# A pool-and-retention decoder step: two independent panels put into each head of the sample stage, states loaded one by one

## What is computed

```python
h = rmsnorm(x, g_norm)
u_p, z_p, q, k, v, z_r, gates = split(h @ w_in)            # w_in: 1024 x 10240
pooled = window_mean(u_p with 15 old rows, 2/4/8/16) - u_p # four groups of 256 columns
y_pool = ((pooled @ w_pool_group) * pool_scale * silu(z_p)) @ w_branch_pool
for each of 4 heads:                                       # q, k: 256 wide, v: 512 wide
    o, s_new = retention(rope(q), rope(k), v, state_ret)   # state: 8 sequences x 256 x 512
    y_ret += (group_norm(o) * gn_ret * silu(z_r)) @ w_branch_ret
merged = sigmoid(gate_p) * y_pool + sigmoid(gate_r) * y_ret
y_sample = rmsnorm(x + merged @ w_out, g_final)
```

## Time and profile before

| | us |
|---|---|
| median of 3 runs | 3111.87 (3109.57 to 3117.58) |
| the profiled execution, its own time | 3111.35 |
| its span, first to last instruction | 3109.7 |
| mean granted TensorE clock | 0.989 |
| PE busy | 2991.4 (96%) |
| sample stage, first panel to last instruction | 2783.36 to 3103.0 |

### The profile page before, as it was taken

The page is one execution under the profiler, slowest core; times in us unless marked ns, Lnnn a source line. Parts: engine busy times, 40 slices in busy tenths (PEclk is TensorE's granted clock), DMA queues, the critical chain, the costliest instruction groups (busy, mean ns, idle before and its releaser), DMA issues.

```text
span 3109.7 us, 36004 instructions
## 1 busy us (share of the span) xinstructions
PE 2991.4 (96%) x13000; PEld 2305.5 (74%) x13000; DVE 1826.3 (59%) x2594; ACT 1152.4 (37%) x1892; POOL 712.1 (23%) x499
## 2 busy tenths in 40 slices
PE   6999999999999999999998999999999999999997
PEld 5888887877778888887887788788888888772222
DVE  7666665764454656666664674657567566754331
ACT  4444443444454444443443333333334332322210
POOL 4252535343332334343432000000000000001110
PEclk8999999999999999999999999999999999999999
DMA  4535353435553354444445546735654663559895
GB/s 131 198 127 190 124 195 129 176 122 183 178 175 122 136 177 148 165 159 150 156 162 220 223 163 246 276 121 193 242 193 161 237 270 140 193 173 336 298 310 190
DMA packets 297599, 582.06 MB, mean 187 GB/s; under 512 B 24840, under 2 KB 167688, under 8 KB 286255
## 3 DMA queue, kind: packets, MB, share of 16 engines
q1 hardware_dynamic: 292039, 562.73, 51.1%
q0 software_dynamic: 5392, 17.12, 1.5%
HBM read 410.63 MB, written 169.50 MB: 187 GB/s over the span
## 4 chain that ended last, share of the span: by engine, by line
PE 84%; DVE 7%; DMA 3%; issue 3%; ACT 2%; POOL 1%; SPq 0%; DVEq 0%; ACTq 0%; POOLq 0%
PE bank L1134 24%; PE bank L1136 24%; PE bank L1135 24%; PE bank L1426 7%; PE bank L1464 2%; PE bank L1182 1%; DMA raw<-in_w_branch_pool 1%; DVE z_in L2123 1%; DVE wa_lo L1857 1%; DMA xs<-in_x_prompt 1%; DVE z_lo L1857 1%; PE bank L1457 1%; DVE win_a L1857 1%; PE bank L1129 1%; DVE c_out L1857 1%
## 5 line engine op out<-in xcount | busy, mean ns | idle before, releaser
L1134 PE MATMUL bank<-xa_hi,wa_hi 128*128 128x512 f32 x2240 | 887.4, 396 | 16.4 <-DVE c_out L1857 11.8
L1136 PE MATMUL bank<-xa_hi,wa_lo 128*128 128x512 f32 x2240 | 877.2, 392 | 0.0
L1135 PE MATMUL bank<-xa_lo,wa_hi 128*128 128x512 f32 x2240 | 876.5, 391 | 0.0
L1134 PEld LDWEIGHTS bank<-xa_hi,wa_hi 128*128 128x128 f32 x2240 | 423.5, 189 | 103.8 <-issue 19.2
L1136 PEld LDWEIGHTS bank<-xa_hi,wa_lo 128*128 128x128 f32 x2240 | 423.0, 189 | 89.2
L1135 PEld LDWEIGHTS bank<-xa_lo,wa_hi 128*128 128x128 f32 x2240 | 423.8, 189 | 85.1
L1857 DVE TENSOR_TENSOR wa_lo<-w_raw,wa_hi 128x512 fp32r<-128x512 f32 x320 | 308.9, 967 | 209.0 <-ACT wa_hi L1559 207.9
L1857 DVE TENSOR_TENSOR wa_lo<-w_sum,wa_hi 128x512 fp32r<-128x512 f32 x240 | 189.4, 789 | 226.7 <-ACT wa_hi L1559 226.7
L1857 DVE TENSOR_TENSOR w_lo<-raw,w_hi 128x512 fp32r<-128x512 f32 (+1 forms) x288 | 180.0, 658 | 228.1 <-ACT w_hi L1665 228.0
L1559 ACT ACTIVATE wa_hi<-w_raw 128x512 fp32r<-128x512 f32 x320 | 201.1, 628 | 243.4 <-PE bank L1136 243.4
L1665 ACT ACTIVATE w_hi<-raw 128x512 fp32r<-128x512 f32 (+1 forms) x288 | 165.5, 603 | 280.3 <-PE bank L1136 108.5
(11 more groups left out here) (238 smaller groups left out, 4606.8 us busy)
## 6 DMA issues: line engine op xcount, KB each, us to landing
w_raw<-in_w_in SPq DMA_DIRECT2D x80, 1024.0 KB, 5.1
v_d<-turned SPq DMA_DIRECT2D x64, 512.0 KB, 3.2
qk_s<-qk_d SPq DMA_DIRECT2D x32, 1024.0 KB, 7.0
v_s<-v_d SPq DMA_DIRECT2D x32, 1024.0 KB, 10.8
raw<-in_w_branch_ret SPq DMA_DIRECT2D x128, 256.0 KB, 4.2
s_w<-in_w_in SPq DMA_DIRECT2D x64, 512.0 KB, 5.0
tabs<-in_c_rope SPq DMA_DIRECT2D x16, 1024.0 KB, 5.2
qk_d<-high SPq DMA_DIRECT2D x32, 512.0 KB, 4.5
```

The costliest lines, as they stand in the source:

```text
L1134: pe.matmul(out, lh, rh, start=first, stop=False, skip_group_check=onto)
L1135: pe.matmul(out, lh, rl, start=False, stop=False, skip_group_check=onto)
L1136: return pe.matmul(out, ll, rh, start=False, stop=last, skip_group_check=onto)
```

## The change

- PE, ACT, DVE and POOL write out the loop over heads; thresholds become constants and the `waited` increments go.
- Two panels from the part after the heads stand in each head between z and the transposes of `s_og`: u0, u1 in head 0, zp0, zp1 in head 1, gp0, gp1 in head 2, gr0, gr1 in head 3 (banks 2 and 0). The transposes of u stand behind v of head 1, the pool groups' product behind v of head 3, the transposes of `s_mix` ahead of those of `s_og` in head 3. ACT and DVE get the work on these results in the same heads.
- SP loads states of the next head one by one, each behind the ACT step that scaled its old buffer: four ahead of this head's branch loads, four behind them. So the next head's states stand ahead of its qk and v loads. The gate bias and pool scale are loaded at the end of head 0.
- PE's waits for `fills` and `hist_copied` stand ahead of head 0's first panel, once, and no more behind each v panel.

```diff
@@ semaphore places
+PANELS = []
+for _h, _others in enumerate((("u0", "u1"), ("zp0", "zp1"), ("gp0", "gp1"), ("gr0", "gr1"))):
+    PANELS += [("qk", _h), ("v", _h)] + [("mix", None)] * (_h == HEADS - 1) + [("z", _h)]
+    PANELS += [(name, None) for name in _others] + [("br", _h)]
+PANELS += [(name, None) for name in ("bp0", "bp1", "out0", "out1")]
...
@@ SyncE
+            def load_states(h, some):
+                for q in some:
+                    if h:
+                        sp.wait_ge(s_act.sem, s_act.done("head", h - 1, f"scaled{q}"))
+                    src = io["state_ret"][0, q, h].rearrange("(k p) v -> p k v", p=P)
+                    sp.dma_start(s_in[:, q], src).then_inc(s_state_in[q], 16)
...
+            load_states(0, seqs)
             for h in range(HEADS):
                 if h:
                     load_qkv(h)
-                sp.wait_ge(s_act.sem, s_act.done("head", h, None))
-                for q in seqs:
...
+                if h == HEADS - 1:
+                    for k in range(4):
+                        load_pair(pair("mix", None, k), io["w_pool_group"][0, k], GW)
+                load_columns("z", h, h * DV + COL_ZR)
+                for p in range(2):
+                    name, first = (("u", COL_U), ("zp", COL_ZP), ("gp", COL_G), ("gr", COL_G + D))[h]
+                    load_columns(f"{name}{p}", None, first + 512 * p)
+                if h + 1 < HEADS:
+                    load_states(h + 1, range(4))
                 for p in range(2):
                     for k in range(2):
...
+                if h + 1 < HEADS:
+                    load_states(h + 1, range(4, SB))
+                if h == 0:
+                    sp.wait_ge(out_stored, 16 * NT * NB)
...
@@ PE
-            with pe.Fori(0, HEADS) as h:
-                panel(h, SQK, 4, sx, P)
-                panel(h, SV, 5, sx, P)
-                pe.wait_ge(fills, 5)
-                pe.wait_ge(hist_copied, 2)
+            pe.wait_ge(fills, 5)
+            pe.wait_ge(hist_copied, 2)
+            for h in range(HEADS):
+                panel("qk", h, 4, sx, P)
+                panel("v", h, 5, sx, P)
+                if h == 1:
+                    wait("head", 0, "other1", s_act)
+                    transposes(6, s_u[:], KT).then_inc(s_mm.sem, 1)
+                if h == HEADS - 1:
+                    wait("head", h - 1, "y1")
+                    wait("head", 1, f"pooled{GROUPS - 1}")
+                    for g in range(GROUPS):
...
                 wait("head", h, "rope5")
-                pe.sem_inc(waited, 1)
...
+                panel("z", h, 6, sx)
+
+                other = ("u", "zp", "gp", "gr")[h]
+                panel(f"{other}0", None, 2, sx)
+                wait("head", h, "new7_1")
+                panel(f"{other}1", None, 0, sx)
+                if h == HEADS - 1:
+                    wait("head", h, "mixed1")
+                    transposes(7, s_mix[:], KT).then_inc(s_mm.sem, 1)
                 wait("head", h, "og")
-                pe.sem_inc(waited, 1)
                 transposes(6, s_og[:], 4).then_inc(s_mm.sem, 1)
                 wait("head", h, "og_t")
+                wait("head", h, "other0", s_act)
...
@@ DVE, between s_og and s_ogt
+                if h == 1:
+                    sample_windows()
+                for p in range(2):
+                    w = slice(p * 512, (p + 1) * 512)
+                    bank = banks[(2, 0)[p]][0:S, :]
+                    if h == 1:
+                        wait("head", h, f"other{p}", s_act)
+                        st(s_z[:, w], bank, s_z[:, w], ALU.mult)
+                    elif h > 1:
+                        dve.wait_ge(s_gate_in, 32)
+                        used(("gp", "gr")[h - 2] + str(p), None)
+                        st(s_g[:, 2 * h - 4 + p, :], bank, s_gate_b[:, 2 * h - 4 + p, :], ALU.add)
                 wait("head", h, "og_t", s_mm)
```

More of the change, by code:

```diff
@@ L170, with __init__, in_heads @@
     credit = 1
-    def __init__(self, sem, once, head, tail):
-        self.sem, self.names = sem, {"once": once, "head": head, "tail": tail}
-        self.length = {k: len(v) for k, v in self.names.items()}
-    def done(self, part, h, name):
[L177 to L181, removed]
+    def __init__(self, sem, once, heads, tail):
+        self.sem, self.at = sem, {}
+        n = self.credit
+        for part, h, names in [("once", 0, once)] + [("head", h, heads[h]) for h in range(HEADS)] + [("tail", 0, tail)]:
+            self.at[part, h, None] = n
+            for name in names:
+                n += 1
+                self.at[part, h, name] = n
+    def done(self, part, h, name):
+        return self.at[part, h, name]
+def in_heads(names, **at_head):
+    lists = []
+    for h in range(HEADS):
+        own = []
+        for name in [None] + names:
+            if name:
+                own.append(name)
+            for heads, more in at_head.get(name or "first", ()):
+                if h in heads:
+                    own += more
+        lists.append(own)
+    return lists
 def build(nc, io):
@@ L461, in build @@
         seqs = range(SB)
-        s_pow = Steps(sem("s_pow"), ["x"], ["o"], ["out"])
-        s_stored = Steps(sem("s_stored"), [], ["states"], [])
+        s_pow = Steps(sem("s_pow"), ["x"], in_heads(["o"]), ["out"])
+        s_stored = Steps(sem("s_stored"), [], in_heads(["states"]), [])
         s_mm = Steps(sem("s_mm"), ["x_t", "hist"],
-                     ["qk_t", "scores"] + [f"update{q}" for q in range(6)] + ["o", "update6", "update7", "og_t"],
-                     ["u_t", "pg_t", "m_t"])
+                     in_heads(["qk_t", "scores"] + [f"update{q}" for q in range(6)]
+                              + ["o", "update6", "update7", "og_t"],
+                              first=(((1,), ["u_t"]),), update7=(((3,), ["pg_t"]),)), ["m_t"])
@@ L471, in build @@
         s_dve = Steps(sem("s_dve"), ["var", "x", "hist0", "hist1"],
[L472 to L476, removed]
@@ L481, in build, with pair, loads @@
+                      ["gate_y0", "gate_y1", "m_gated0", "m_added0", "m_gated1", "m_added1", "x0", "x1", "var", "final"])
+        def pair(name, h, k=0):
+            return 4 * PANELS.index((name, h)) + k
+        def loads(m):
+            return sum(2 if PANELS[i // 4][0] == "qk" else 1 for i in range(m % SRING, m + 1, SRING))
         w_in = io["w_in"][0]
@@ L968, in _ @@
[L968 to L981, removed]
+                        load_pair(pair("br", h, 2 * p + k),
+                                  io["w_branch_ret"][0][h * DV + k * 2 * P:h * DV + (k + 1) * 2 * P, p * 512:(p + 1) * 512])
@@ L1107, in _ @@
                 pool.sem_inc(s_stored.sem, 1)
[L1108 to L1111, removed]
+                if h == 0:
+                    pool.wait_ge(s_act.sem, s_act.done("head", 0, "other1"))
+                    for q in seqs:
+                        pool.dma_start(io["pool_sample"][0, q, HIST - ST:HIST, :], s_u[q * ST:(q + 1) * ST, :])\
+                            .then_inc(s_rest_out, 16)
             inverse_std("tail", 0, "var")
@@ L1413, in _, with unit @@
             pe.wait_ge(out_squared, KT * NB)
[L1415 to L1423, removed]
+            def unit(name, h, k, bank, lhs, first, last, at_col=0, width=512):
+                m = pair(name, h, k // 2)
                 if k % 2 == 0:
-                    pair_loaded(h, n)
-                mm = pe.matmul(banks[bank][0:lhs.shape[-1], at_col:at_col + width], lhs, s_w[:, n % SRING, k % 2, 0:width],
+                    pe.wait_ge(s_w_in[m % SRING], 16 * loads(m))
+                mm = pe.matmul(banks[bank][0:lhs.shape[-1], at_col:at_col + width], lhs, s_w[:, m % SRING, k % 2, 0:width],
                                start=first, stop=last)
@@ L1503, in _ @@
             wait("tail", 0, "m_t", s_act)
-            panel(None, SOUT0, 2, s_mt)
-            panel(None, SOUT1, 3, s_mt)
+            panel("out0", None, 2, s_mt)
+            panel("out1", None, 3, s_mt)
         @block.scalar
@@ L1818, in scaled @@
                 do(s_out[:, q % 4], s_in[:, q], scale=s_decay[:, 0:1])
-            with act.Fori(0, HEADS) as h:
+            for h in range(HEADS):
                 wait("head", h, "rope5")
@@ L2324, in _, with used, sample_windows, sample_mix @@
             dve.wait_ge(fills, 5)
-            def used(h, n):
-                dve.wait_ge(s_w_used, (HEADS if h is None else h) * PH + n + SRING)
-            with dve.Fori(0, HEADS) as h:
-                used(h, SQK + 4)
+            def used(name, h, pairs=4):
+                dve.wait_ge(s_w_used, SRING + pair(name, h, pairs))
+            def sample_windows():
+                src, dst, valid = s_ext, s_wa, 0
+                for g in range(GROUPS):
+                    wait("head", 1, f"window{g - 1}" if g else "u_t")
+                    d = 1 << g
+                    valid += d
+                    st(dst[:, 2 * g:, :, valid:], src[:, 2 * g:, :, valid:], src[:, 2 * g:, :, valid - d:20 - d], ALU.add)
```

(51 more changed lines are left out.)

173 lines of the change are left out of this document (69 added, 104 removed).

## The result

The changed kernel takes 3130.34 us in the median (3122.36 to 3132.27, 5 runs), the kernel before 3117.58 beside it (3109.57 to 3124.04, 5 runs). The ratio is 1.0042, 95% interval 1.0022 to 1.0062: 13 us slower (7 to 19), where I had forecast 1.3 us and a time within 0.3%. The profiled execution, the fastest of the five, took 3122.36 us with a span of 3120.6.

A forecast was written before the change was run, and what follows sets the result against it. PE, busy 96% of the span, bounds the kernel: only its gaps, clock and entry waits can move. Gains of 19.6 us against losses of 20.9 gave 1.3 us slower, 3113 us in the median, range 3102 to 3122.

The forecast's parts named there:

- The gap for `s_og`: Between z and branch product in each head: two panels fill PE's gap, 12.5 us before, 4.6 after; 7.9 us won.
- Its slow stretch: The 48 matmuls behind the `s_og` gap in each head: no lower clock behind the shorter gaps; 6.0 us won.
- After the heads: `s_mix` work moves inside head 3's state updates, so its gap and the slow stretch behind it go; 4.6 us won.
- Constants: Waits in the loop over heads: constant thresholds save at two places per head; 1.1 us won, bounds 0 and 8.
- The entry: Head 0's first panel: PE waits for `hist_copied`, 7.3 us lost, plus 1.2 for a slow stretch; together 8.5.
- The loads of qk: Heads 1 to 3: qk loads queue behind states and branch loads; PE waits 9.0 us in all, bounds 5 and 14.
- Slow stretches behind the waits: Behind the qk waits of heads 1 to 3: 1.7 us each, 3.4 us lost, bounds 0 and 5.1.
- The prediction's own sign of this: Sign of being wrong, in the sample stage: waits at branch or v panels too, then the time is over 3121.
- The second rival: Sample stage: qk loads flow at less than 386 GB/s, the queue falls further behind; edge 3121, example 3126; chance 0.13.

The follow-up runs named there:

- both edits: Changed kernel with the entry's waits behind head 0's v panel and all next-head states behind its qk and v: 3094.86 us, ratio 0.9935 to the kernel before.
- the small stores: Changed kernel with each new state's store cut to 64 of its 512 columns: one execution, 3112.76 us.
- the early wait alone: Kernel before with PE's waits for `fills` and `hist_copied` once, ahead of head 0's first panel: 3130.14 us, ratio 1.0040.

## Why the prediction was wrong

Step by step, in the stage's profile.

1. *The gap for `s_og`: right.* With loads out of the way, in the kernel with both edits, PE resumes 0.81, 1.65, 1.11 and 0.62 us (1.31 less the moved transposes) behind the second panel; I had 0.9, 1.75, 1.1 and 0.8. Won: 12.5 - 4.2 = 8.3 us, for 7.9.
2. *Its slow stretch: right.* None stands behind these gaps in the kernel with both edits: every branch product takes 7.05 us. 6.0 us.
3. *After the heads: right.* bp0 follows the last branch product at once, the four operations on `s_mix` show nowhere. 4.6 us.
4. *Constants:* 1.8 us less of waits, nothing in the time. I had 1.1.
5. *The entry: the wait right, the slow stretch too small.* 7.5 us against 7.3. But the clock took 2.8 us in the first two panels, for my 1.2 and above my upper bound of 1.7.
6. *The loads of qk: mechanism right, size off.* This is the term that failed. I had PE wait 4.0, 2.15 and 2.8 us, 9.0 in all. It waited 13.5 for qk and, beyond `s_ogt`, 2.01 - 0.81, 2.16 - 1.65 and 1.23 - 1.11 = 1.8 for branch pairs that I had called just met: 15.3. Three parts of it. The broadcasts of gate bias and pool scale, costed by bytes at 1.0 us, took 3.2. The first qk pair landed near Z + 33.7 and Z + 32.8 in heads 1 and 2, for 31.9: from Z + 6.4 on the queue moved 370 and 377 GB/s, where I had taken the 386 of a full stretch before, and some 19.3 and 19.0 transfers' worth of bytes went by before the pair was there, for my 18.8. And the branch pairs came at Z + 22.7, 22.9 and 21.9, for the Z + 21 that I had rounded to "just met" and put at no cost.
7. *Slow stretches behind the waits:* 1.5 + 0 + 1.7 = 3.2 us, for 3.4. But they fell elsewhere too: 1.7 in head 1's branch product and 1.7 in the first state products of head 0 and of head 2 each, 5.1 us in no step of mine. Those of head 0 can't be put down to the early wait: with the entry's waits back behind v they took 5.32 us in one kernel and 3.62 in the one with both edits.

Gains 8.3 + 6.0 + 4.6 + 1 = 20, losses 7.5 + 2.8 + 15.3 + 8.3 = 34: 14 us, for the 13.3 of the traces. My forecast had 20.9 us of losses. The range's upper end took step 6 and 7 at their bounds or the rival of a slower queue, but not together with a dearer entry and slow stretches elsewhere. The prediction's own sign of this came true: waits at the branch panels too, and then over 3121.

The absolute time was off by more than these terms. Of the 17 us between 3113 and the median of 3130.34, 9.7 are what the traces differ by beyond my 1.3. The other 8, less the 0.5 that I had allowed, are the distance from the profiled execution to the median. The kernel before moved alike, from 3111.87 in three runs to 3117.58 in five; my range held nothing for that.

The second rival was the nearest. It put its edge at waits of 15.3 us and a first pair at Z + 34.0, which is almost what came, but by a slower queue alone. The queue was slower (370 and 377 GB/s), but that is only a part; the broadcasts and the branch pairs are the rest, so the sum fits it partly by luck. The page DMA: Bandwidth & Descriptors of the Trainium skill, section Specifications, would have had 358 GB/s; the 370 and 377 of the trace lie between it and my 386. Its 15 us of waits are near by the same luck. What the same page says of taking turns between rings (section Queues, rings and completion order) fits the small stores, which delay loads on another ring; they don't show the turns themselves.

What stays open: why the clock's grants fall behind gaps of a third of a microsecond in heads 0 and 2 and not in 1 and 3. Across these runs the same gaps were followed by either, in different heads. No run holds everything else and moves the stage by a chosen amount, so that it goes with the shift of the whole is a guess.

## What to carry to other kernels

In a queue served in its order of issue, ask of each transfer what it stands ahead of. Here eight state loads per head that were needed last went out first, and PE waited 15 us more; behind the weights, at an unchanged byte count, PE waited for no load. Before work is moved to fill a gap, look at what a hoisted wait is released by: one wait lifted from behind two panels, where it had long been met, to ahead of them held PE for 7.5 us more, and cost 8 to 12 us by the medians or ratios of three pairs of kernels.

## What the runs showed of the hardware

- Two broadcast loads, 384 KB together to 32 rows, held up the queue like 1.2 MB: 3.2 us, 261 GB/s at a DMA share of 1.09.
- A 512 KB store on POOL's queue delayed the loads on SP's by most of what a load would: cut to an eighth, three of them let the first qk pair land 3.2, 2.6 and 2.0 us earlier.
- In the changed kernel and its variants the branch product took 7.03 to 7.05 us behind idle times of up to 1.58 us, and 8.71 or 8.72 behind 1.73, 1.78, 1.80 and 2.06. A qk panel behind 2.19 us ran undisturbed, right behind one of these slow products. No run sets the idle time by itself.
- The same PE gap of 2.2 us was followed by a product that took 8.75 us in one kernel and 9.94 in another, 7.0 being undisturbed; and state products behind small gaps took 3.55 or 5.25 us. So a gap has no fixed price. The kernel before spread over 17 us in 31 runs and the one with the early wait alone over 20 in 10, while the one with both edits spread over 6 in 6.
